# Low parts of the mixed heads on GpSimd, second copies of the turned weights on VectorE

## What is computed

```python
proj = rmsnorm(h, norm1_g) @ w_in
# attention head, a block of 128 queries:
z = q @ k.T * scale
log_beta = log_sigmoid(z)
log_one_minus = where(visible, log_sigmoid(-z), 0)
later = reversed_cumsum(log_one_minus) - log_one_minus
w = where(visible, exp(log_beta + later), 0)
o_sb = group_rmsnorm(w @ v)
mix = concat([o_sb, o_hg]) @ w_out
h = h + mix
h = h + (silu(u2 @ w_gate) * (u2 @ w_up)) @ w_down      # u2 = rmsnorm(h, norm2_g)
```

## Time and profile before

| | us |
|---|---|
| median of 3 runs (lowest, highest) | 1410.84 (1410.66, 1414.07) |
| the profiled execution | 1416.32 |
| its span in the profile | 1414.6 |
| TensorE busy | 1331.5 (94%) |
| VectorE busy | 816.9 (58%) |
| ScalarE busy | 550.7 (39%) |
| GpSimd busy | 44.0 (3%) |

### The profile page before, as it was taken

How to read it: one execution, slowest core, us unless ns; L and a number is a source line. 1 busy time by engine, 2 the same in 40 slices (tenths; PEclk the granted TensorE clock), 3 DMA queues, 4 the chain that set the end, 5 groups by cost and what they waited for, 6 DMA issues and landing times.

```text
span 1414.6 us, 23813 instructions
## 1 busy us (share of the span) xinstructions
PE 1331.5 (94%) x9812; PEld 1116.2 (79%) x9812; DVE 816.9 (58%) x1351; ACT 550.7 (39%) x1015; POOL 44.0 (3%) x64
## 2 busy tenths in 40 slices
PE   5999999999999999689859999999999998999997
PEld 5898989897667667489858888888888876888886
DVE  5376776773787475932467655665566545435423
ACT  6323233222575555921354333333333324324411
POOL 3000000000000000010140000000000000000000
PEclk8999999999999999999989999999999999999999
DMA  6211111010010000040312222122222129615601
GB/s 196 60 31 31 31 31 32 31 53 9 2 47 16 31 2 27 6 165 31 116 64 89 87 85 82 64 86 90 89 90 90 60 82 370 213 65 201 237 23 60
DMA packets 79548, 112.24 MB, mean 79 GB/s; under 512 B 3776, under 2 KB 57024, under 8 KB 79440
## 3 DMA queue, kind: packets, MB, share of 16 engines
q1 hardware_dynamic: 77728, 104.94, 22.3%
q0 software_dynamic: 1712, 5.78, 1.1%
HBM read 90.78 MB, written 19.92 MB: 78 GB/s over the span
## 4 chain that ended last, share of the span: by engine, by line
PE 89%; ACT 5%; DVE 2%; DMA 2%; issue 2%; SPq 1%; ACTq 0%; DVEq 0%; POOLq 0%
PE ps L1912 10%; PE ps L1915 10%; PE ps L1914 10%; PE ps L313 8%; PE ps L315 8%; PE ps L314 8%; PE ps L1985 5%; PE ps L1986 5%; PE ps L1987 5%; PE ps L997 3%; PE ps L325 2%; PE ps L326 2%; PE ps L327 2%; PE ps L960 2%; PE ps L601 2%; PE ps L977 2%
## 5 line engine op out<-in xcount | busy, mean ns | idle before, releaser
L313 PE MATMUL ps<-a_hi,w_hi 128*128 128x352 f32 (+2 forms) x576 | 208.2, 362 | 7.7 <-DVE a_lo L429 3.2
L314 PE MATMUL ps<-a_lo,w_hi 128*128 128x352 f32 (+2 forms) x576 | 200.5, 348 | 0.0
L315 PE MATMUL ps<-a_hi,w_lo 128*128 128x352 f32 (+2 forms) x576 | 200.4, 348 | 0.0
L313 PEld LDWEIGHTS ps<-a_hi,w_hi 128*128 128x128 f32 x576 | 109.5, 190 | 20.5 <-DVE a_lo L429 3.6
L315 PEld LDWEIGHTS ps<-a_hi,w_lo 128*128 128x128 f32 x576 | 109.5, 190 | 8.4
L314 PEld LDWEIGHTS ps<-a_lo,w_hi 128*128 128x128 f32 x576 | 109.7, 190 | 7.3
L1912 PE MATMUL ps<-a_hi,w_hi 128*128 128x512 f32 x288 | 112.7, 391 | 2.6 <-DVE a_lo L1631 2.6
L1985 PE MATMUL ps<-a_hi,w_hi 128*128 128x512 f32 x288 | 112.1, 389 | 2.2 <-DVE a_lo L1776 2.2
L1915 PE MATMUL ps<-a_hi,w_lo 128*128 128x512 f32 x288 | 112.8, 392 | 0.0
L1914 PE MATMUL ps<-a_lo,w_hi 128*128 128x512 f32 x288 | 112.7, 391 | 0.0
L1987 PE MATMUL ps<-a_hi,w_lo 128*128 128x512 f32 x288 | 112.0, 389 | 0.0
(11 more groups left out here) (262 smaller groups left out, 2660.9 us busy)
## 6 DMA issues: line engine op xcount, KB each, us to landing
w_raw<-in_w_in_dram SPq DMA_DIRECT2D x24, 512.0 KB
w_raw<-in_w_gate_dram SPq DMA_DIRECT2D x11, 1024.0 KB, 5.6
h_res<-in_w_up_dram SPq DMA_DIRECT2D x11, 1024.0 KB, 5.4
f_spill<-h_res SPq DMA_DIRECT2D x44, 256.0 KB, 2.0
h_norm<-f_spill SPq DMA_DIRECT2D x44, 256.0 KB, 4.3
w_raw<-in_w_down_dram SPq DMA_DIRECT2D x22, 512.0 KB, 5.2
h_res<-in_w_down_dram SPq DMA_DIRECT2D x22, 512.0 KB, 5.3
mixed<-in_x_dram SPq DMA_DIRECT2D x8, 512.0 KB, 7.5
```

The source lines that it names most:

```text
L313: nc.tensor.matmul(psum, wh, ah, start=k == 0, stop=False)
L314: nc.tensor.matmul(psum, wh, al, start=False, stop=False)
L315: last = nc.tensor.matmul(psum, wl, ah, start=False, stop=k == KT - 1)
```

## The change

The second copies of pieces 42 to 53 go from ScalarE to VectorE. The sixteen low parts of `mixed` go from VectorE's extras to GpSimd's queue, where all sixteen stand ahead of the reload of x (L1301) and of the gain (L1303). The high parts, and what TensorE waits for, stay.

```diff
         NP = len(PIECES)
-        SCALAR_COPIES = range(3 * PER_PAIR, NP - 2)
+        SCALAR_COPIES = range(0)
...
-        def split_vector(dve, t, half):
-            dve.wait_ge(m_hi.sem, m_hi.done(SPLITS.index((t, half)) + 1))
-            nc.vector.tensor_tensor(tok_lo[:, t, X_PARTS[half]], mixed[:, t, X_PARTS[half]],
+        def split_pool(pool, t, half):
+            pool.wait_ge(m_hi.sem, m_hi.done(SPLITS.index((t, half)) + 1))
+            nc.gpsimd.tensor_tensor(tok_lo[:, t, X_PARTS[half]], mixed[:, t, X_PARTS[half]],
                                     tok_hi[:, t, X_PARTS[half]].bitcast(F32), ALU.subtract).then_inc(m_lo.sem, 1)
...
                     if n - 1 - part in CHUNK_AT:
                         low_chunk(dve, CHUNK_AT[n - 1 - part], part)
-                for t, half in SPLIT_AT.get(n, []):
-                    split_vector(dve, t, half)
...
                 last.then_inc(fills.sem, 1)
+                for t, half in SPLITS:
+                    split_pool(pool, t, half)
                 pool.wait_ge(av_evac.sem, av_evac.done(8))
                 for t in range(TT):
                     pool.dma_start(h_res[:, t, :], x2[t * P:(t + 1) * P, :]).then_inc(x_back[t].sem, 16)
...
                 head_norm_widen(dve, 7)
                 head_norm_finish(dve, 7, bank(7))
-                for t, half in SPLITS[15:]:
-                    split_vector(dve, t, half)
```

## The result

The changed kernel takes 1424.78 us (median of 4 runs, 1423.46 to 1426.44) beside 1411.13 for the kernel before (4 runs, 1410.66 to 1414.07): a ratio of 1.0093 with an interval of 1.0075 to 1.0111. It is slower, by 13.1 us. The ratio weighs all runs and is not the quotient of the two medians, which differ by 13.65 us. On another chip the ratio was 1.0109 (1.0096 to 1.0122), from 4 runs of the changed kernel beside 23. The forecast was 1421.3 with a range of 1411 to 1427.

What follows compares the result with a forecast made beforehand. VectorE and ScalarE were taken to bound the last pair of heads, TensorE nearly everything else. Projection start +9.1 us and reload wait +1.4 made +10.5 on 1410.84: 1421.3 us, range 1411 to 1427.

Steps and rivals of the forecast that it cites:

- the first rival: Last pair of heads: GpSimd holds only VectorE's products, not its scans; -0.2 us, 1410.6 us, no change; chance 0.13.
- no exclusion: Last pair: GpSimd slips into gaps without holding VectorE; projection earlier, -6.5 + 1.4 = -5 us, 1406 us; chance 0.07.
- Starvation of GpSimd: Last pair: VectorE keeps the port and GpSimd begins only near 599.5 us; +7.4 + 1.4, 1419.6 us; chance 0.05.
- VectorE's bare work, 30.0 us: Last pair: VectorE's own work unheld, 34.2 - 8.4 (low parts leaving) + 4.15 (copies coming) = 30.0 us.
- The exclusion, 15 x 1.24 less 2.5, 16.1 us: Last pair: fifteen GpSimd subtractions each hold VectorE for 1.24 us, 18.6 us, less 2.5 beside copies or lulls.
- the discount for copies and lulls: Last pair: 2.5 us taken off 18.6 for GpSimd work beside a VectorE copy or lull; bounds 0 and 6.5.
- the price of 1.24: Last pair: VectorE's cost per GpSimd subtraction, 2.44 - 1.20 us, read from two VectorE subtractions at 740.92.
- The 2.4 us in hand: End of the last pair: spare time after VectorE's last products, 604.23 to 606.62 us, taken to be used up.
- The reload, +1.4: Output projection, fifth group: TensorE waits 1.4 us as x's reload stands behind the sixteenth GpSimd low part; upper end 4.0.
- The sum of +10.5: Whole kernel: last pair +9.1 us plus +1.4 us of waiting for the reload of x, put on the 1410.84 median.

## Why the prediction was right, and where it was not

**The mechanism held.** GpSimd's subtractions shut out scans and products of VectorE, and the copies out of PSUM not. The scans, which no row had shown beside GpSimd, are held (1294 ns for 956), so the first rival falls; "no exclusion" falls with the same rows and with the run in which GpSimd only writes, which does gain, 3.29 us in the last pair where that rival had put -6.5 (its own numbers give 569.5 + 30.0 + 4.24 = 603.7, that is -7.0). Starvation of GpSimd falls: no subtraction in the last pair is over 2.19 us.

**VectorE's bare work, 30.0 us: right.** With the copies alone the stretch has the length that the terms add up to.

**The exclusion, 15 x 1.24 less 2.5, 16.1 us: too much, and mostly in the price.** VectorE's stretch goes from 569.09 to 612.1, 43.0 us, and 43.0 - 30.0 = 13.0. By form: 2.7 + 1.9 + 1.8 + 1.0 = 7.4 us on scans (eight of 384, six of 400, eight of 272, two of 512 columns) and 3.2 + 1.0 + 1.0 = 5.2 on products. So a subtraction cost 0.87 us on average, and 5.6 us came off the 18.6 instead of 2.5. It would be easy to blame the discount for copies and lulls. The run with the low parts alone says otherwise: without the moved copies a subtraction already costs 0.99, so 3.7 us (15 x 0.25) are the price of 1.24, and the copies' cover is the remaining 1.9, close to the 2.5 taken. The 1.24 was a misreading of the two VectorE subtractions at 740.92; apart they are

```profile
740.92 0.82 DVE L1657 TENSOR_TENSOR w_lo<-h_res,w_hi 128x512 fp32r<-128x512 f32 x1 [1.22 <-ACT w_hi L1380]
741.67 1.77 DVE L1657 TENSOR_TENSOR w_lo<-h_res,w_hi 128x512 fp32r<-128x512 f32 x1
```

The first was held for 0.14 us by the end of one GpSimd subtraction and the second for 1.09 by a whole one: two meetings, charged as one. In the changed kernel, too, the longest surcharges are about this much, 1.01 on a scan of 384 columns (1.97 us at 579.94) and 1.07 on a product of 383 (1.61 at 583.31). So a whole subtraction costs 1.0 to 1.1 us, and what meets VectorE in part costs less.

**The 2.4 us in hand: they were not there.** I took the time from the last products (604.23) to the turning of piece 55 (606.62) for slack. Before that turning TensorE does the values of 54, which need VectorE's copy of 54, and that copy stands behind the weighing of 55. Only 604.23 to 605.11 was free of it. From the end of that weighing to the projection it takes 6.7 us (612.1 to 618.80), not 4.24. About 1.5 of the 2.4 us is the order: the copy and the values of 54, from 605.11 to 606.62 before, can't start until VectorE is through. From that copy on it took 5.65 us before (605.11 to 610.76) and takes 6.77 now (612.03 to 618.80); these 1.1 us are the clock, 1.0 of them in values and turning (1.55 and 0.91 us in place of 0.88 and 0.59).

These two errors have opposite signs, -3.1 and +2.4 us, and VectorE started 0.4 us before the assumed 569.5. That the projection's start came out within 1.0 us (618.80, forecast 619.8) is in good part luck.

**The reload, +1.4: measured 1.80 and 2.54.** Mechanism and place were as told; the first landing took 4.2 and 4.9 us instead of 3.9. The run with the reload first takes the wait away.

**Missing: TensorE's clock.** In the first 10.94 us of the projection the granted clock was 0.72, in the same stretch before 0.81. The two levels are 1.2 and 2.4 GHz, and the profile's 0.72 is a mix of them. Ahead of it, in the last pair, TensorE was busy for 32.51 of 54.35 us at a mean clock of 0.84, before the change for 30.38 of 45.89 at 0.90. Over the whole second stretch the clock makes 0.8 us in one profiled execution of the change and 2.7 in the other, beside 2.1 us more of TensorE's busy time in the last pair, which its waits cover in part. The sum of +10.5 lacked this term. In the second execution it is most of the way from 10.5 to the 13.8 of both stretches; in the first both stretches give 11.0. The 2.1 and 1.6 us from there to the timed +13.1 and +15.4 lie in neither stretch of these executions, and where they come from is open. So is how much of the clock the change brings in every execution: of two one had 0.8 and the other 2.7, and the low level also appears in executions of the kernel before (0.81 above).

**The range** had to reach to the second execution's case, and did: the medians of 1424.78 and, scaled to the first chip, about 1426 lie in its upper part. The likeliest value was 3.5 us too low. In the two traced stretches the shortfall is 0.5 and 3.3 us, made of the landing and the clock, less the 0.6 us by which the last pair grew less than forecast; the rest isn't placed.

## What to carry to other kernels

Work put on an idle GpSimd is not hidden when it reads SBUF beside a VectorE that has no gaps with two-SBUF-input work: price it near its own duration on VectorE as an upper bound (here a subtraction of 1.27 us cost 0.99 on average, and 0.87 where copies out of PSUM gave cover), and don't let it queue up several instructions deep ahead of a VectorE instruction that TensorE waits for. Before calling the end of an engine's work slack, walk through every engine's written order up to the next stage. When two engines are full in one stage, look first for work that can move to the next stage: of all versions here that compute the same only that one gained, by 0.11%.

## What was not expected of the hardware

VectorE and GpSimd did not always alternate. In the last pair a VectorE instruction waited for about one subtraction (scans and products up to 2.2 us, four of GpSimd's in 6.82 us). Behind the reload a single one waited for everything queued, 7.64, 7.49 and 7.79 us, for three different forms, while the seven subtractions ran at 1.24 us each, undisturbed. Before the change, at 740.92, VectorE had got in after one. And the same L1050, in the changed kernel's last pair, met two subtractions queued from 599.09 to 602.15 and got in after the first:

```profile
600.36 0.66 DVE L1050 COPY gain<-small 128x512 f32<-128x512 f32 x1
```

What separates the cases isn't settled. The Trainium skill, in the section named above, has it that issue order and not the shape of the instruction decides who blocks; the three forms agree, but it speaks of one instruction's length, and here it was seven's. The prediction gave that section's rule without the exception it makes for VectorE's 2-port modes, which copies within SBUF can enter; L1050 has a single SBUF input and was held all the same, and which mode it ran in no run here shows. A reciprocal of 128x8, one SBUF input, went through at 612.34 beside the same queue in 0.20 us.
